# Attention with forget gates, two heads at a time: scores on halves of TensorE's rows, values on halves of its columns

## The reference

```
z = h @ w_in
q, k, v, f_logit, gate = split_cols(z, ODD_SPLITS)
log_cum = jnp.cumsum(log_sigmoid(f_logit + b_f), axis=1)
s = einsum('bqhd,bkhd->bhqk', qi, k) * scale          # 128 queries, all keys
s = s + ci[..., :, None] - lc_t[..., None, :]         # the decays
s = where(mask, s, -inf);  p = softmax(s)
o = einsum('bhqk,bkhd->bqhd', p, v)
return x + (o * silu(gate)) @ w_out
```

## Time and profile before

| | |
|---|---|
| median of 3 runs | 3001.79 us |
| profiled execution, its span | 2985.12 us, 2983.8 us |
| PE, DVE, ACT busy | 93%, 33%, 21% of the span |
| share of PE in the chain that ended last | 86% |
| fox layer: projections of pair 0 | from about 735 us |
| fox layer: steps | from about 789 to 1531 us |

### The profile page before, as it was taken

The page is one execution under the profiler, slowest core; times in us unless marked ns, Lnnn a source line. Parts: engine busy times, 40 slices in busy tenths (PEclk is TensorE's granted clock), DMA queues, the critical chain, the costliest instruction groups (busy, mean ns, idle before and its releaser), DMA issues.

```text
span 2983.8 us, 31038 instructions
## 1 busy us (share of the span) xinstructions
PE 2770.6 (93%) x12382; PEld 1839.7 (62%) x12382; DVE 992.2 (33%) x2562; ACT 631.0 (21%) x1622; POOL 137.2 (5%) x156
## 2 busy tenths in 40 slices
PE   7899899999999999999999999988899889699993
PEld 4688667744577667766754566644464655577662
DVE  4344414513132223222332446664400234411114
ACT  3343323401122223222321111110000210011111
POOL 1000000000000000000000000000000000012212
PEclk9999999899999999999999999999999999699997
DMA  4000100322100111001041200004140122358865
GB/s 142 28 1 1 60 12 1 86 85 64 29 22 8 29 29 29 1 1 57 1 109 61 67 32 25 32 0 148 49 169 0 57 87 99 131 166 234 227 171 160
DMA packets 145910, 202.23 MB, mean 68 GB/s; under 512 B 18016, under 2 KB 102880, under 8 KB 145760
## 3 DMA queue, kind: packets, MB, share of 16 engines
q1 hardware_dynamic: 138592, 175.01, 18.1%
q0 software_dynamic: 7168, 25.17, 3.8%
HBM read 162.27 MB, written 37.75 MB: 67 GB/s over the span
## 4 chain that ended last, share of the span: by engine, by line
PE 86%; DVE 6%; ACT 2%; issue 1%; DMA 1%; POOL 0%; DVEq 0%; POOLq 0%; ACTq 0%; SPq 0%
PE banks L168 79%; PE banks L171 6%; PE banks L2497 1%; ACT arena L1288 1%; DVE arena L1938 0%; DVE arena L2572 0%; DMA x_scratch<-arena,places 0%; DVE arena L1016 0%; DVE arena L2723 0%; DVE arena L1020 0%; DVE arena L2721 0%; ACT arena L981 0%; ACT arena L2155 0%; DVE arena L1584 0%; ACT arena L672 0%
## 5 line engine op out<-in xcount | busy, mean ns | idle before, releaser
L168 PE MATMUL banks<-arena 128*128 128x512 f32 (+12 forms) x10190 | 2582.4, 411 | 56.4 <-DVE arena L1908 9.1
L168 PEld LDWEIGHTS banks<-arena 128*128 128x128 f32 (+2 forms) x10190 | 1619.1, 193 | 881.0 <-issue 751.9
L171 PE MATMUL banks<-arena 128*128 128x128 f32 (+1 forms) x1744 | 282.7, 284 | 87.2 <-DVE arena L425 16.0
L171 PEld LDWEIGHTS banks<-arena 128*128 128x128 f32 (+1 forms) x1744 | 216.8, 148 | 169.4 <-issue 79.9
L661 ACT ACTIVATE arena<-banks,arena 128x128 f32<-128x128 f32 (+3 forms) x192 | 142.2, 741 | 333.5 <-DVE arena L686 332.4
L686 DVE TENSOR_REDUCE arena<-banks 128x1 f32<-128x128 f32 (+3 forms) x192 | 145.5, 758 | 153.3 <-PE banks L168 151.4
L250 POOL TENSOR_TENSOR arena<-arena 128x1 f32<-128x1 f32 (+1 forms) x88 | 57.7, 658 | 2539.6 <-DVE arena L1139 1566.0
L698 DVE COPY arena<-banks 128x512 f32<-128x512 f32 (+2 forms) x144 | 76.0, 528 | 274.7 <-PE banks L171 274.4
L707 DVE SCALAR_TENSOR_TENSOR arena<-banks,arena 128x64 f32<-128x64 f32 x192 | 54.4, 283 | 229.3 <-PE banks L168 228.1
L727 DVE SCALAR_TENSOR_TENSOR arena<-arena,banks 128x128 f32<-128x128 f32 x128 | 35.9, 281 | 145.1 <-ACT arena L723 145.1
L1288 ACT ACTIVATE arena<-banks 64x512 f32<-64x512 f32 x64 | 38.0, 593 | 192.7 <-PE banks L168 192.3
(11 more groups left out here) (252 smaller groups left out, 1170.6 us busy)
## 6 DMA issues: line engine op xcount, KB each, us to landing
x_scratch<-arena SPq DMA_DIRECT2D x40, 512.0 KB, 2.8
arena<-in_o_w_in_dram SPq DMA_DIRECT2D x32, 512.0 KB, 6.9
arena<-x_scratch SPq DMA_DIRECT2D x32, 512.0 KB, 5.6
arena<-in_w_gate_dram SPq DMA_DIRECT2D x16, 1024.0 KB, 14.2
arena<-in_w_up_dram SPq DMA_DIRECT2D x16, 1024.0 KB, 16.2
arena<-in_w_down_dram SPq DMA_DIRECT2D x16, 1024.0 KB, 7.4
arena<-in_x_dram SPq DMA_DIRECT2D x16, 512.0 KB, 4.5
arena<-in_w_in_dram SPq DMA_DIRECT2D x16, 512.0 KB, 7.3
```

The source lines that it names most:

```text
L168: return pe.matmul(o, a, b, start=start, stop=stop)
L171: return pe.transpose(o, a, ident)
```

## The change

Scores of both heads of a pair are made in one step, each on one half of TensorE's rows (64 rows: the decay rows are gone), with the queries negated, and a negated identity `identn` adds the mask. The decays of the keys are stored to DRAM once, and each head's row is loaded over all 128 partitions (`NB`, 512 KB a head). VectorE's one instruction `tensor_tensor_reduce` adds it to the scores, writes the sum to SBUF and gives the row's minimum. ScalarE takes the exponential from SBUF. The turned weights of four tiles are gathered in `PTF`; then the values, 64 columns wide, are the stationary operand, and up to 512 columns of turned weights stream against them, head 0 to partitions 0 to 63 and head 1 to partitions 64 to 127 of bank 6. The gates, divided by the row sums, are turned four tiles at once, and VectorE multiplies by them. A step is now a tile of both heads, 64 in all; a unit of v and gate takes two tiles, so that a pair has 8 units. The weights of the pairs use two buffers in place of three. Cut to its core:

```diff
+identn = ctx.enter_context(nc.sbuf_tensor("identn", [128, 128], BF16))
...
+fw = [tiled(weights(f"fox {p}", (1, 3)[p % 2], 4), 8) for p in range(8)]
...
-QA = [scr(4 * i, 1024) for i in range(4)]
-KF = [scr(16 + 4 * i, 1024) for i in range(4)]
-VG = [tiled(scr(32 + 8 * i, 2048), 8) for i in range(2)]
-PT_F = [scr(56, 1024), WR[0][:, 0:1024]]
+QF = [scr(4 * i, 1024) for i in range(2)]
+KF = [scr(8 + 4 * i, 1024) for i in range(2)]
+VG = [tiled(scr(16 + 8 * i, 2048), 8) for i in range(2)]
+NB = [tiled(scr(32 + 8 * i, 2048), 2) for i in range(2)]
+PF = [[scr(48, 1024), scr(52, 1024)], [XB[0], XB[1]]]
+GRo = tiled(scr(56, 512), 4)
+GRT = scr(58, 512)
+PTF = [tiled(WR[0], 8), tiled(WR[2], 8)]
...
+def load_decays(p):
+    for h in range(2):
+        load(NB[p % 2][:, h, :], row(decays[2 * p + h]), d_aug[p % 2])
...
-    load_fox(1)
 def sp_fox():
     Y.wait_ge(proj_done, out1.proj + NT)
-    load_fox(2)
+    load_fox(1)
     Y.wait_ge(decay_done, 2)
+    sync.dma_start(decays, LC[0:16, :]).then_inc(d_decays.sem, 16)
+    Y.wait_ge(d_decays, 16)
+    load_decays(0)
+    load_decays(1)
     for p in range(8):
-        par = p % 2
-        if p >= 2:
-            Y.wait_ge(s_done, fox.s + 16 * (p - 1))
-        for h in range(2):
-            b = 2 * par + h
-            load(QA[b][64:65, :], LC[2 * p + h:2 * p + h + 1, :], d_aug[b])
-            load(KF[b][65:66, :], NLC[2 * p + h:2 * p + h + 1, :], d_aug[b])
-        if p >= 1 and p + 2 < 8:
-            Y.wait_ge(f_pe, fox.f + 12 * p)
+        Y.wait_ge(f_pe, fox.f + 8 * (p + 1))
+        if p + 2 < 8:
             load_fox(p + 2)
-    Y.wait_ge(f_pe, fox.f + 84)
+        if 1 <= p < 7:
+            Y.wait_ge(mx_done, fox.mx + 16 * p)
+            load_decays(p + 1)
+        if p == 6:
+            load_k(w_o2[1], o_w_out[0][:, 512:1024], d_w[1])
     load_k(w_o2[0], o_w_out[0][:, 0:512], d_w[3])
-    load_k(w_o2[1], o_w_out[0][:, 512:1024], d_w[1])
...
-        t = j - 4
-        for k in range(NK):
-            m = mm(zb[:, 0:256], HT[:, k, 128 * t:128 * t + 128], fw[q][:, k, 256:512], k == 0, k == 7)
+        for half in range(2):
+            t = 2 * (j - 4) + half
+            for k in range(NK):
+                m = mm(zb[:, 256 * half:256 * half + 256], HT[:, k, 128 * t:128 * t + 128], fw[q][:, k, 256:512],
+                       k == 0, k == 7)
...
-        for h in range(2):
-            m = act.activation((QA, KF)[w][2 * (q % 2) + h][0:64, 512 * n:512 * n + 512],
-                               zb[64 * h:64 * h + 64, :], ACT.Copy, scale=(0.125, 1.0)[w])
-        m.then_inc(f_a.sem, 1)
+        act.activation((QF, KF)[w][q % 2][:, 512 * n:512 * n + 512], zb, ACT.Copy,
+                       scale=(-0.125, 1.0)[w]).then_inc(f_a.sem, 1)
     else:
-        t = j - 4
-        C.wait_ge(pv_done, fox.pv + 16 * (q - 1))
-        act.activation(VG[q % 2][:, t, 0:128], zb[:, 0:128], ACT.Copy, scale=0.5)
-        act_gate(zb[:, 128:256], 8 * q + t, fox.g + 8 * q + t - 1)
...
+        t, z3 = 2 * (j - 4), tiled(zb, 2)
+        C.wait_ge(pv_done, fox.pv + 2 * (q - 1))
+        act.activation(VG[q % 2][:, t:t + 2, 0:128], z3[:, :, 0:128], ACT.Copy, scale=0.5)
+        C.wait_ge(gate_done, fox.g + 4 * q + j - 5)
+        act.activation(tiled(GE[j % 2], 2), z3[:, :, 128:256], ACT.Tanh, scale=0.5).then_inc(f_a.sem, 1)
...
+        V.wait_ge(p_turned, fox.t + 26 * (q - 1))
+        vec.scalar_tensor_tensor(VG[q % 2][:, t:t + 2, 128:256], tiled(GE[j % 2], 2), 1.0,
+                                 tiled(fox_bank(q, j), 2)[:, :, 128:256], ADD, MUL).then_inc(gate_done.sem, 1)
...
+    P.wait_ge(ex_done, fox.ex + 2 * i + h + 1)
+    for c in range(1 + t // 4):
+        tb = fox.bank_free(("p", i, h, c))
+        for j in range(min(4, t + 1 - 4 * c)):
+            b = 4 * c + j
+            m = tr(tb[:, 128 * j:128 * j + 128], PF[i % 2][h][:, 128 * b:128 * b + 128])
+        m.then_inc(p_turned.sem, 1)
...
-    pe_attention(fox, fox_q, fox_k, fox_v, PT_F, filler)
+    P.wait_ge(f_a, fox.fa + 8)
+    P.wait_ge(gate_done, fox.g + 3)
+    for s in range(64 + 2):
+        if s < 64:
+            p, t = s // 8, s % 8
+            n = 128 * (t + 1)
+            P.wait_ge(f_a, fox.fa + 8 * p + 4)
+            P.wait_ge(mx_done, fox.mx + 2 * s)
+            for b in range(0, n, 512):
+                w = min(512, n - b)
+                for h in range(2):
+                    mm(bank(2 * h, 2)[:, b:b + w], QF[p % 2][64 * h:64 * h + 64, 128 * t:128 * t + 128],
+                       KF[p % 2][64 * h:64 * h + 64, b:b + w], True, b + w != n)
+            for h in range(2):
+                mm(bank(2 * h, 2)[:, n - 128:n], identn[:, :], maskq[:, :], False, True).then_inc(s_done.sem, 1)
+        if s >= 2 and (s - 2) % 4 == 3:
+            g = (s - 2) // 4
+            p, last = g // 2, 4 * (g % 2) + 3
+            P.wait_ge(og_done, fox.og + g)
+            for i in range(4 * g, 4 * g + 4):
+                for h in range(2):
+                    for c in range(1 + i % 8 // 4):
+                        fox.emptied(P, ("p", i, h, c))
+            for b in range(last + 1):
+                lo = 128 * max(0, b - last + 3)
+                for h in range(2):
+                    m = mm(bank(6)[64 * h:64 * h + 64, lo:512], VG[p % 2][:, b, 64 * h:64 * h + 64],
+                           PTF[h][:, b, lo:512], b == 0, b == last)
+            m.then_inc(pv_done.sem, 1)
+        if 1 <= s <= 64:
+            pe_fox_turn(s - 1, 0)
+        if s < 56:
+            q, j = s // 8 + 1, s % 8
+            P.wait_ge(f_a, fox.fa + s + 8)
+            P.wait_ge(gate_done, fox.g + 4 * q + max(j - 4, 0))
+            pe_fox_unit(q, j)
+        if 1 <= s <= 64:
+            pe_fox_turn(s - 1, 1)
+            if s % 4 == 0:
+                g = s // 4 - 1
+                P.wait_ge(gr_done, s)
+                tb = fox.bank_free(("o", g))
+                for m_ in range(4):
+                    m = tr(tb[:, 128 * m_:128 * m_ + 128], GRo[:, m_, :])
+                m.then_inc(p_turned.sem, 1)
...
+    for s in range(64 + 1):
+        if s < 64:
+            n, a8 = 128 * (s % 8 + 1), at8[s % 6]
+            for h in range(2):
+                C.wait_ge(mx_done, fox.mx + 2 * s + h + 1)
+                act.activation(PF[s % 2][h][:, 0:n], PF[s % 2][h][:, 0:n], ACT.Exp, bias=a8[:, h:h + 1], scale=-1.0,
+                               accum_out=a8[:, 2 + h:3 + h]).then_inc(ex_done.sem, 1)
...
-    for i in range(4):
-        vec.memset(QA[i][64:66, :], 1.0)
-        vec.memset(KF[i][64:66, :], 1.0)
...
-    for j in range(12):
-        dve_fox_filler(0, j)
+    vec.tensor_scalar(identn[:, :], identb[:, :], -1.0, None, MUL).then_inc(decay_done.sem, 1)
...
+    for s in range(64 + 2):
+        if s < 64:
+            p, n, a8 = s // 8, 128 * (s % 8 + 1), at8[s % 6]
+            V.wait_ge(d_aug[p % 2], 32 * (p // 2 + 1))
+            for h in range(2):
+                V.wait_ge(s_done, fox.s + 2 * s + h + 1)
+                if s >= 2:
+                    fox.turned(V, ("p", s - 2, h, (s - 2) % 8 // 4))
+                vec.tensor_tensor_reduce(PF[s % 2][h][:, 0:n], NB[p % 2][:, h, 0:n], bank(2 * h, 2)[:, 0:n], 1.0, BIG,
+                                         ADD, MIN, a8[:, h:h + 1]).then_inc(mx_done.sem, 1)
...
+            V.wait_ge(ex_done, fox.ex + 2 * i + 2)
+            vs(vec.reciprocal(a8[:, 4:6], a8[:, 2:4]))
...
+            vec.tensor_tensor(tiled(GRo[:, i % 4, :], 2), tiled(VG[p % 2][:, t, 128:256], 2),
+                              a8[:, 4:6].rearrange("p (h c) -> p h c", c=1).to_broadcast([128, 2, 64]),
+                              MUL).then_inc(gr_done.sem, 1)
...
+            V.wait_ge(pv_done, fox.pv + g + 1)
+            fox.emptied(V, ("o", g))
+            vec.tensor_tensor(OT[:, g // 2, 512 * (g % 2):512 * (g % 2) + 512], bank(6), GRT, MUL).then_inc(og_done.sem, 1)
...
+        if s < 56:
+            dve_fox_unit(s // 8 + 1, s % 8)
```

More of the change, by code:

```diff
@@ L194, in program @@
         w_o1 = [tiled(weights("out 1a", 3, 1), 8), tiled(weights("out 1b", 0, 1), 8)]
-        fw = [tiled(weights(f"fox {p}", 1 + p % 3, 4), 8) for p in range(8)]
+        fw = [tiled(weights(f"fox {p}", (1, 3)[p % 2], 4), 8) for p in range(8)]
         w_o2 = [tiled(weights("out 2a", 3, 1), 8), tiled(weights("out 2b", 1, 1), 8)]
@@ L1304, in pe_fox, with fox_turned_out @@
+        def fox_turned_out(eng, i, h):
+            t, m = i % 8, i % 4
+            for c in range(1 + t // 4):
+                key = ("p", i, h, c)
+                if fox.by_act(key) == (eng is C):
+                    w = min(4, t + 1 - 4 * c)
+                    fox.turned(eng, key)
+                    eng.wait_ge(pv_done, fox.pv + i // 4)
+                    yield PTF[h][:, 4 * c:4 * c + w, 128 * m:128 * m + 128], tiled(bank(4 + fox.turn[key] % 2)[:, 0:128 * w], w)
         def pe_fox():
@@ L1306, in pe_fox @@
             pe_forget(1)
-            for j in range(12):
+            for j in range(8):
                 if j >= 2:
@@ L1312, in pe_fox @@
```

(31 more changed lines are left out.)

105 lines of the change are left out of this document (71 added, 34 removed).

## The result

The changed kernel takes **2881.11 us** (median of 4 executions, 2878.51 to 2883.95), the kernel before 3002.51 beside it (2988.21 to 3009.83). The ratio is 0.960, 95% interval 0.956 to 0.964. The forecast of 2932 had the right sign, and both overlaps that it rests on show in the trace; the time lies under its range of 2900 to 2990. The profiled execution took 2883.95 us with a span of 2882.6, against 2985.1 and 2983.8.

What follows compares the result with a forecast made beforehand. TensorE, busy 93% of the span, was taken to bound the kernel. Seven filled pairs (-87.5), the last pair (+1) and its half clock (+17) sum to -69.5 us: 3001.8 becomes 2932, range 2900 to 2990.

Steps and rivals of the forecast that it cites:

- both overlaps: Per filled pair: two heads' scores stream together on row halves, gain 4.5 us; values on column halves, gain 7.0.
- going in and out: TensorE switching between full-array work and half-array streams: 0.41 us lost each time, bounds 0 and 0.8.
- the rivals on the columns: Value groups: halves one after the other, 11 us, chance 0.12; or loads not hidden, 7 to 8 us, chance 0.10.
- the page's figure: For column halves: the skill's 2.38 times for three column tiles, by estimate about 1.6 times for two.
- The gain of a filled pair: Each of seven pairs with fillers: scores 4.5, values 7.0, waits 1.0; 12.5 us a pair, 87.5 in all.
- The eight units of 3.51 us: Projections of 256 columns in a pair; with four units of 6.92 us they were costed at 55.8 us.
- Waits: TensorE idle in a pair, 2.1 us; ScalarE emptying q and k in one instruction gives back about 1.0.
- The last pair: Pair 7, without fillers: 52 us at full clock against 50.9 before, +1; near 69 at half clock.
- The half clock: TensorE's clock at half from the third step of pair 7, slowing scores, turns and last values: +17 us.
- the row of swa: Swa layer without fillers: PE busy 9.2 of 11 us, clock halved within 10 us, scores 1.23 us instead of 0.70.
- The base: Starting time 3001.8 us, the median of the runs, 16.7 us above the profiled run and left so.

Runs made afterwards that it cites:

- x_cols_turn: The changed kernel with all value blocks of head 0 ahead of head 1's, still on column halves; 2933.96 us, ratio 0.981.
- x_between: The changed kernel with one full-array bf16 mask more between the two chunks' scores, 4 a pair; 2892.26 us.
- x_after: The changed kernel itself, unedited, timed and profiled again; 2879.16 us.
- x_before: The kernel before the change, unedited, timed and profiled again; 2997.51 us, ratio 1.002.
- x_last_fill2: The changed kernel with two wide matmuls that nobody reads added in each of steps 58 to 63, in the last pair; 2877.27 us.
- x_rows_turn: The changed kernel with the two heads' scores one after the other, each closed by its mask; 2956.69 us, ratio 0.988.

## Why the prediction had the overlaps right and the number wrong

- **Which engine, and both overlaps: right.** PE fills a filled pair (83.6 of 84.0), and the longest wait in one is 0.39 us. Undone by themselves, each overlap gives back 7.7 us of streams a pair (+9.98 for the rows with a second going in and out, +7.26 for the columns without any). Against the kernel before, scores gained 5.5 us and values 7.3, where 4.5 and 7.0 were forecast; the rivals on the columns (11 us a group, or 7 to 8 with loads in the open) are refuted by 5.74. The Trainium skill ("TensorE: Matmul & The Clock Gate", Part 3, "What overlaps and what doesn't") lets a load overlap a running matmul only where row groups differ; here both column halves share all rows, and 5.74 us for 5.59 of stream leaves 0.15 for the 16 loads of each half. The trace decides against the rule. In turn (x_cols_turn) the group takes 10.72 us, 1.87 times as long; the prediction's estimate from the page's figure was 1.6.
- **The gain of a filled pair, 12.5: it was 14.75.** Going in and out was put at 0.41 us from swa and is 0.29 to 0.30 (x_between): 8 x 0.12 = 1.0. A group of values pays 0.15 over its stream and about 0.1 ahead, not 0.41: 0.3. The eight units of 3.51 us now go by twos, in four of 6.91, and those of 6.92 take 6.87: 55.1 in place of 55.8, 0.7. Waits are what is left of 84.02, 0.8 us of 2.1: they gave back 1.3, not 1.0, 0.3. Together that is 2.3, for the 2.25 by which the forecast fell short, and **15.8 us** in seven pairs. The terms that were mis-sized are thus above all the price of the halves, taken from swa, and the units.
- **The first pair: 6.3 us forgotten.** The last pair was charged with the value group and turns that slide into it from pair 6. The same slide takes them out of pair 0, whose gain is 21.1, not 12.5; the sum credited it nowhere.
- **The last pair: the step that failed in kind.** Work at full clock was right: 52 forecast; 55.3 measured with 10.2 us at half clock, by estimate some 4 us of loss (3.79 - 1.99 for the scores, about as much again on the turns), so near 51. The half clock was wrong: taken for the whole pair from its third step, +17, by the row of swa. In the profiled execution it was there for 6.8 and 3.4 us only, beside the two waits of 3 us. It was the largest miss of one term, **13.6 us** (forecast +18, measured +4.4).
- **Outside the steps of fox** 4.0 us came on top. All but 0.4 are the execution's and not the change's: x_after, the same kernel, takes 3.6 less there, with 15 us less at half clock.
- **The base.** Against profiled executions the forecast misses 31.7 us: 15.8 + 6.3 + 13.6 - 4.0 = 31.7. The other 19.2 are the 16.4 us added (rounded) for the median of before, and the changed kernel's median lying 2.8 *under* its profile. x_before shows what the first most likely was: half clock for 30.7 us in its last pair, 13 us longer. None of nine executions of the changed kernel lies that far from the others, though its last pair is thinner. Why the clock falls in the old last pair in some executions only, with PE 93% busy in the profile without a fall (47.4 of 50.9 us), stays open; in x_last_fill2 more work in the new one's waits went with a clock that stayed up, but what sets the falls is not shown.

## What to carry to other kernels

In f32, cost two half-array streams as one stream plus 0.3 us for every time that full-array work stands between them, and check the order of the queue as well as the tiling: in these runs the halves had to alternate within two f32 matmuls. When work slides from one stage to the next, credit the stage it leaves. Before a median is taken for a base, look at whether the profiled execution and the median had the same granted clock.

## What was not expected of the hardware

- **Reach of the overlap.** One or two f32 matmuls of one half in a row lose next to nothing (84.02, 84.11), four lose 3.3 us a pair, all eight 6.5. The Trainium skill ("TensorE: Matmul & The Clock Gate", Part 3, "The mechanism") gives a reorder window 64 deep, in which loads are pulled ahead of running matmuls. What these runs show is another thing and shorter: for column halves, each block with loads of its own, a matmul pass of the other half starts at most about four passes ahead of its turn.
- **A full-array mask of 0.06 us costs 0.36** between half-array matmuls (x_between), and with one between the heads the whole overlap is gone (x_rows_turn).
- **10.3 us of work that nobody needs cost nothing in sum** in a pair with 13.1 us of waits (x_last_fill2 against x_after): 6.5 went into the waits, and the clock's falls were gone from the profiled execution.
